# A three-attention transformer stack on one core: query and key groups are drained in two pieces

## What is computed

```python
p = h @ w_in
qa, ka, va, ga, qs, ks, vs, gs, qf, kf, vf, gf, ff = jnp.split(p, split_at, axis=-1)
ya = merge(diff_attention(qa, ka, ...)) ; ya = ya * jax.nn.silu(ga)      # 4 heads, difference of two softmaxes
yb = merge(stick_breaking_attention(qs, ks, vs)) ; yb = yb * jax.nn.silu(gs)   # 8 heads
yc = merge(forgetting_attention(qf, kf, vf, cum_log_f)) ; yc = yc * jax.nn.silu(gf)   # 8 heads
y = jnp.concatenate([ya, yb, yc], axis=-1) @ w_out
return x + rms_norm(y, g_post)
```

## Time and profile before

| what | value |
|---|---|
| median of 3 runs | 1998.19 us (1995.54 to 2000.15) |
| the profiled execution's own time | 1998.55 us |
| its span, first to last instruction | 1996.7 us |
| PE busy | 1897.4 us, 95% of the span |
| ACT, DVE, POOL busy | 906.2, 778.3, 661.8 us |
| mean granted clock of TensorE | 0.988 |

### The profile page before, as it was taken

The page is one execution under the profiler, slowest core; times in us unless marked ns, Lnnn a source line. Parts: engine busy times, 40 slices in busy tenths (PEclk is TensorE's granted clock), DMA queues, the critical chain, the costliest instruction groups (busy, mean ns, idle before and its releaser), DMA issues.

```text
span 1996.7 us, 24926 instructions
## 1 busy us (share of the span) xinstructions
PE 1897.4 (95%) x9233; PEld 1546.8 (77%) x9239; DVE 778.3 (39%) x1346; ACT 906.2 (45%) x1775; POOL 661.8 (33%) x278
## 2 busy tenths in 40 slices
PE   8998999898999899989899999999999999999998
PEld 6887777676788777777676888888788878888886
DVE  3434655534543565544447672010350431111002
ACT  4555565543465556554353833233453353323222
POOL 2422333122242222322233444434103423444442
PEclk9998999999999899999999999999999999999999
DMA  4221212112322121211231222222102422222322
GB/s 153 85 74 43 74 65 74 53 43 106 116 85 66 51 72 66 74 53 43 104 138 65 95 95 95 86 94 89 60 1 75 142 78 97 95 95 95 99 101 85
DMA packets 44568, 163.74 MB, mean 82 GB/s; under 512 B 6192, under 2 KB 6448, under 8 KB 43824
## 3 DMA queue, kind: packets, MB, share of 16 engines
q1 hardware_dynamic: 42640, 148.65, 22.3%
q10 hardware_dynamic: 1824, 13.63, 1.8%
HBM read 155.97 MB, written 6.29 MB: 81 GB/s over the span
## 4 chain that ended last, share of the span: by engine, by line
PE 82%; DVE 9%; ACT 6%; issue 3%; DMA 0%; POOL 0%; DVEq 0%; ACTq 0%; POOLq 0%; SPq 0%
PE bank L644 12%; PE bank L646 12%; PE bank L645 12%; PE bank L647 10%; PE bank L649 10%; PE bank L648 10%; PE bank L771 2%; PE bank L788 2%; ACT q_dup L1013 2%; PE bank L749 1%; PE bank L747 1%; PE bank L750 1%; DVE y_tok L1398 1%; PE bank L735 1%; PE bank L708 1%
## 5 line engine op out<-in xcount | busy, mean ns | idle before, releaser
L627 POOL TENSOR_TENSOR w_hl<-w_raw,w_hl 128x1024 fp32r<-128x1024 f32 x274 | 661.6, 2419 | 1310.6 <-ACT w_hl L899 1310.0
L899 ACT ACTIVATE w_hl<-w_raw 128x1024 fp32r<-128x1024 f32 x274 | 287.6, 1058 | 343.7 <-DMA w_raw<-wstream 343.2
L644 PE MATMUL bank<-act_hl,w_hl 128*128 128x512 f32 x1056 | 428.4, 406 | 5.7 <-DVE q_low L1368 2.8
L646 PE MATMUL bank<-act_hl,w_hl 128*128 128x512 f32 x1056 | 415.4, 393 | 0.0
L645 PE MATMUL bank<-act_hl,w_hl 128*128 128x512 f32 x1056 | 415.1, 393 | 0.0
L647 PE MATMUL bank<-w_hl,act_hl 128*128 128x512 f32 x672 | 265.6, 395 | 6.1 <-DVE q_low L1368 4.0
L649 PE MATMUL bank<-w_hl,act_hl 128*128 128x512 f32 x672 | 262.3, 390 | 0.0
L648 PE MATMUL bank<-w_hl,act_hl 128*128 128x512 f32 x672 | 262.0, 390 | 0.0
L644 PEld LDWEIGHTS bank<-act_hl,w_hl 128*128 128x128 f32 x1056 | 201.1, 190 | 48.9 <-issue 5.7
L646 PEld LDWEIGHTS bank<-act_hl,w_hl 128*128 128x128 f32 x1056 | 200.2, 190 | 43.5
L645 PEld LDWEIGHTS bank<-act_hl,w_hl 128*128 128x128 f32 x1056 | 201.1, 190 | 40.3 <-issue 1.9
(11 more groups left out here) (232 smaller groups left out, 2839.7 us busy)
## 6 DMA issues: line engine op xcount, KB each, us to landing
w_raw<-wstream SPq DMA_DIRECT2D x274, 512.0 KB, 3.5
x_spill<-x_res ACTq DMA_DIRECT2D x2, 2048.0 KB, 7.0
x_res<-x_spill ACTq DMA_DIRECT2D x2, 2048.0 KB, 7.9
x_res<-x SPq DMA_DIRECT2D x4, 512.0 KB, 5.7
g_post<-post_gains ACTq DMA_DIRECT2D x4, 512.0 KB, 3.6
x_res<-x ACTq DMA_DIRECT2D x1, 2048.0 KB, 8.4
out<-x_res SPq DMA_DIRECT2D x4, 512.0 KB, 2.6
probs<-w_gates ACTq DMA_DIRECT2D x1, 1024.0 KB, 10.7
```

The source lines that it names most:

```text
L627: nc.gpsimd.tensor_tensor(w_hl[:, slot, 1].rearrange("p c n -> p (c n)"), w_raw[:, slot, :], w_hl[:, slot, 0].rearrange("p c n -> p (c n)" ...
L644: pe.matmul(out_ap, wh, ah, start=start, stop=False)
L646: return pe.matmul(out_ap, wl, ah, start=False, stop=stop)
L899: nc.scalar.activation(w_hl[:, b % RING, 0].rearrange("p c n -> p (c n)"), w_raw[:, b % RING, :], ACT.Copy).then_inc(s_high_done, 1)
```

## The change

The drains of the groups with tag "qk" that are woven into attention are split. A `drain` step now carries its tiles. `halved` puts the piece for the tiles (0, 1) behind the half of the last block that computes them, and the piece for (2, 3) behind the other half. One part of an attention step (at A and D two parts) lies between them. No instruction is added or removed, and PE's queue is the same, row for row, as are those of SP and GpSimd. Lines of the changed kernel's engine functions are 15 higher.

```diff
+SPLIT_DRAINS = ("qk",)
@@ def dense
-        out.append(("drain", len(groups) - 1))
+        out.append(("drain", len(groups) - 1, (0, 1, 2, 3)))
+    def halved(dense_steps):
+
+        out = []
+        for st in dense_steps:
+            if st[0] == "drain" and groups[st[1]]["tag"] in SPLIT_DRAINS:
+                first, second = halves(st)
+                out[-1:] = [first, out[-1], second]
+            else:
+                out += halves(st) if st[0] == "block" else [st]
         return out
@@ ACT and DVE, drain
-                for j in range(4):
+                for j in tiles:
```

More of the change, by code:

```diff
@@ L60, in dense, with halves @@
             blocks.append((len(groups) - 1, k))
-        out.append(("drain", len(groups) - 1))
+        out.append(("drain", len(groups) - 1, (0, 1, 2, 3)))
+        return out
+    def halves(st):
+        return [st[:-1] + ((0, 1),), st[:-1] + ((2, 3),)] if st[0] in ("block", "drain") else [st]
+    def halved(dense_steps):
[6 more added lines that the diff above has]
+                out += halves(st) if st[0] == "block" else [st]
         return out
@@ L67, in weave @@
         for dense_steps, upto in segments:
-            rest = [half for st in dense_steps
-                    for half in ([st[:4] + ((0, 1),), st[:4] + ((2, 3),)] if st[0] == "block" else [st])]
+            rest = halved(dense_steps)
             n, seen = sum(st[0] == "block" for st in rest), 0
@@ L187, in plan @@
             g = groups[st[1]]
-            for j in range(4):
+            for j in st[2]:
                 take(("dense", st[1], j), j, signal=j < 3)
@@ L539, in values_before @@
         for st in STEPS:
-            if st == ("drain", gi):
+            if st[:2] == ("drain", gi):
                 return n
@@ L947, in forget, with drain @@
                 nc.scalar.activation(lam[:, 2:4], lam[:, 0:2], ACT.Exp).then_inc(s_lam_exp, 1)
-            def drain(gi):
+            def drain(gi, tiles):
                 g = GROUPS[gi]
@@ L1167, in _ @@
                 elif st[0] == "drain":
-                    drain(st[1])
+                    drain(st[1], st[2])
                     if st[1] + 1 in LAST:
@@ L1304, in forget, with drain @@
                 dve.wait_ge(s_ck_ready, l + 1)
-            def drain(gi, tiles=range(4)):
+            def drain(gi, tiles):
                 g = GROUPS[gi]
```

## The result

The changed kernel takes 2002.45 us (median of 11 runs, 2000.37 to 2007.37) against 1997.96 us (11 runs, 1995.29 to 2000.85). The medians are 4.5 us apart. Forecast were +6.8 us (2005.0) and slower. The profiled execution took 2001.84 us, its span is 2000.0 us and its mean granted clock 0.983, where 0.988 was.

A forecast was written before the change was run, and what follows sets the result against it. PE, busy 95% of the span, was taken to bound the kernel, so only its stalls and granted clock could matter. Stalls +2.0 and clock +4.8 made +6.8 us, 2005.0 us; forecast range 2001.5 to 2009, overall 1997.5 to 2010.

The forecast's parts named there:

- A: Drain site in "sb", half block 0: PE's wait for bank 7 grows from 0.84 to 4.76 us, +3.9 us.
- D: Drain site in "fox", half block 1: two PE stalls of 6.7 us together replace 7.0 us, -0.3 us.
- The stalls: PE's waits at the four sites and the banks: +1.0 us per layer, +2.0 us for two layers.
- B: Drain site in "sb", half block 1: PE gets its bank at 262.5, wanted at 260.24, +2.3 us.
- C: Drain site in "fox", half block 0: PE's transposes begin at 323.35 and not at 322.55, +0.8 us.
- bank waits: PE's waits for banks 0 and 2 at A, B and C: all six per layer go, -5.6 us.
- The clock at A: Half granted clock behind A's longer stall: 1.6 us taken, a short fall, with 2.6 as upper bound.
- The clock at D: Low granted clock behind D's stalls, which cost 2.4 us before: forecast +0.8 us.
- No new falls: Rival: stalls as forecast, no additional drops to the half clock: +2.0 us, 2000.2 us; chance 0.27 (1995 to 2001.5).
- the strict reading of the Trainium skill: A pause among matmuls is no idleness; only A's stall could cost clock; given the second rival's sum.
- The split pays: Rival, kernel faster: bank waits go, D keeps only its second stall and no fall, 11.7 us per layer, 1974.8 us; chance 0.06.
- ACT's idle time ahead of the map: Test for the faster rival: 1.80 us idle at D, where the piece needs 3.6 us on ACT.

The follow-up runs named there:

- filler_a: The whole change plus 16 unused PE matmuls into bank 4 ahead of the bank 7 wait at A, both layers; ratio 1.0006 against the kernel before.
- d_later: Kernel before, drain split at site D alone, first piece where the whole drain stood, second two parts of attention later; ratio 0.9955.
- A alone: Kernel before with the drain split at site A alone, in both layers, whole at B, C and D; ratio 1.0036.
- head_first: The whole change, but at A DVE takes the instruction freeing bank 7 ahead of the first piece, ACT's order unchanged; ratio 1.0020 against the kernel before.
- only_b: Kernel before with the drain split at site B alone, whole at A, C and D; ratio 1.0004.
- only_d: Kernel before with the drain split at site D alone, placed as in the change, whole elsewhere; ratio 1.0001.

## Why the prediction was right, and where its terms were off

**The stalls** came out within 0.3 us each, since they are only the lengths of instructions put behind one another: A 4.70 us (4.76 forecast), B 2.01 (2.3), C 0.82 (0.8), D 3.35 and 3.23 (3.4 and 3.3), bank waits gone (forecast: all six per layer). The net of +1.0 per layer for the stalls is +0.7 by these rows: 3.86 + 2.01 + 0.82 + 3.35 + 3.23 - 7.02 - 5.6. Two slips in the working change nothing: at A 200.0 is when bank 1 is free (bank 0 is at 198.6, by its own rows), and two thirds of the way to D's scores is 390.5 and not 390.

**The clock at A** was under-sized. I took 1.6 us, the short fall, and called 2.6 the upper bound; the window has 5.30 us of busy time at 0.50, so 2.65 us, and `filler_a` got 2.5 us back at the site in each layer. My reason for the smaller one, that the bank waits behind it are gone, was no reason: the standstill of 4.7 us alone resembled the 3.42 us row and not the 2.23 us row.

**The clock at D** was under-sized too: two falls with 5.66 + 3.20 us of busy time at 0.50 cost 4.4 us for 2.4, so +2.0 and not +0.8. The lag over D says +1.2 to +1.3 with the stalls' -0.4, so +1.6 to +1.7 for the clock, which is less. That part of a low clock can lie where PE would have waited for ACT and DVE anyway is shown for the later piece (`d_later`); for the change it is argued.

**What I had left out** is the other side of that: a later or slower PE meets waits that are then shorter. In the tail of "fox" the change won back 1.4 us per layer: one of the two long waits there, 1.9 us before, is 0.76 us behind a stretch of low clock. The forecast for the stalls was +2.0 us, and PE's idle time as a whole fell by 1.5 us. Site by site, the forecast's terms are about +3.3 at A, +0.9 at B, -1.2 at C and +0.5 at D, and the pairing has +3.6, +0.2, -1.6 and +1.2: the sums are nearly the same, 3.4 to 3.5 per layer, while the terms at A and D were too small and those at B and C too large. That the time came out 1.0 us from the forecast is therefore luck in part: errors of both signs met at the sites, and the forecast had nothing for the places outside them.

**The rivals.** "No new falls" ended at 2001.5 us, 1 us below the median, so the traces decide here and not the time. It was wrong at A in both layers of all three traces in which PE stood still there for 2.9 us or more (the change, A alone, DVE's head first). With it fell the strict reading of the Trainium skill (TensorE: Matmul & The Clock Gate, section "What's actually happening"), by which a pause among matmuls is no idleness: the traces don't agree, since falls stand behind waits of 2.93 us (`head_first`) and 2.01 us (`only_b`, layer 2). The prediction gave that reading the sum of a rival, which is wrong: a fall at A alone and none behind D is +2.0 + 3.2 - 4.8 = +0.4 us. "The split pays" is wrong at A, B and D and right at C. All its bank waits went, 5.6 us per layer, but waits for BT and bank 7 came. ACT's idle time ahead of the map, by which the prediction judged it, isn't what made C pay: there PE has work enough of its own until the map reading behind the piece is nearly done, and waits only 0.82 us.

## What to carry to other kernels

In this kernel, a burst of work that is cut in two helped only where the instruction that another engine waits for isn't put behind the earlier half, or not by more than that engine has to do meanwhile. Look for each piece at the next thing that the busiest engine will want from that queue, and move the half that nobody wants yet later, rather than the other half earlier: at D the earlier first piece left 3.4 + 3.2 us of waits, the later second piece 2.9 + 2.4 or 2.9 + 0.9, and 0.7 to 1.4 us more against 3.1 less. Price a standstill of TensorE with the low clock behind it, which at A was the larger part of the price, and then look at PE's next wait, which can swallow the low clock, as at D in `d_later`.

## What the runs showed of the hardware

A standstill of 2.01 us at B was followed by a granted clock of 0.50 in layer 2 and not in layer 1 of the same execution (`only_b`), and in `filler_a` a fall followed it in both layers. The prediction had left open whether that could be. Nor does a longer standstill always bring a fall: the 3.42 us row of the "diff" tail, which has 0.50 behind it in both layers of the kernel before, has 1.00 behind it in layer 2 of `only_b` and of `only_d` and in layer 1 of `head_first`. In `only_b`:

```profile
681.97 0.66 PE L855 MATMUL bank<-ident,y_tok 128*128 128x128 f32 x4 [3.42 <-DVE y_tok L1513]
```

```profile
682.00:688.00 6.00, 5.81 (x38) 5.02 (x38) 3.62 (x10) 3.59 (x11) 0.00 (x0) 1.00 0.00 0
```

The falls near 469 us and 663 us, too, are present in some executions and missing in others of nearly the same instructions. With one trace for each kernel, no run here shows what decides it.

16 matmuls into an unused bank during the wait at A kept the clock at 1.00 behind it in both layers, and A cost 2.5 us less in each (`filler_a`).
